# A hybrid layer on one core: both output projections with split operands, two tiles at once while the weights come, and x turned inside the second projection

## The reference

```python
mixed = jnp.concatenate([y.astype(x.dtype) * jax.nn.silu(z) for y, z in branches], axis=-1)
return x + mixed @ w_out                  # mixed 2048 x 1280, w_out 1280 x 1024
```

## Time and profile before

| | |
|---|---|
| three runs | 5369.63, 5380.27, 5392.05 us; median 5380.27 |
| the profiled execution | 5369.74 us, its span 5368.1 us |
| TensorE busy over the span | 4420.3 us, 82% |
| DVE, ACT, POOL busy | 2632.6, 1913.5, 738.0 us |
| `po`, first DMA to last product | 2516.99 to about 2844.6 us |
| second projection, first to last product | 2860.6 to about 3514.6 us |
| `pf`, first DMA to last product | 5117.41 to about 5357.5 us |
| POOL remainder of a weight block of `pf` | 2.34 us |

### The profile page before, as it was taken

The page is one execution under the profiler, slowest core; times in us unless marked ns, Lnnn a source line. Parts: engine busy times, 40 slices in busy tenths (PEclk is TensorE's granted clock), DMA queues, the critical chain, the costliest instruction groups (busy, mean ns, idle before and its releaser), DMA issues. The chain is left out here.

```text
span 5368.1 us, 64565 instructions
## 1 busy us (share of the span) xinstructions
PE 4420.3 (82%) x23178; PEld 3238.0 (60%) x23178; DVE 2632.6 (49%) x5352; ACT 1913.5 (36%) x3894; POOL 738.0 (14%) x753
## 2 busy tenths in 40 slices
PE   7988999973678888987998999956688887876668
PEld 6876777762566666665446888833344454544557
DVE  3114444445555544542111111148998888887435
ACT  3112233234223223332111010123676767777511
POOL 3101111100000000000000000012222333444310
PEclk9998999975667677776999999976587887877779
DMA  5336666643010000001221212120000001011032
GB/s 180 124 123 231 210 209 216 215 155 123 24 34 23 23 23 12 23 14 69 85 84 69 81 65 81 54 61 23 17 19 18 18 18 36 18 36 36 30 129 103
DMA packets 199360, 417.95 MB, mean 78 GB/s; under 512 B 37032, under 2 KB 67404, under 8 KB 198876
## 3 DMA queue, kind: packets, MB, share of 16 engines
q1 hardware_dynamic: 199040, 413.81, 22.5%
HBM read 292.08 MB, written 121.65 MB: 77 GB/s over the span
## 5 line engine op out<-in xcount | busy, mean ns | idle before, releaser
L3131 POOL TENSOR_TENSOR ds_E<-ds_bT 128x256 f32<-128x256 f32 x112 | 71.8, 641 | 2928.5 <-ACT ds_bT L3100 2743.2
L2620 PE MATMUL ds_big<-ds_ikT,ds_iqT 64*128 64x512 f32 (+3 forms) x640 | 384.0, 747 | 94.9 <-ACT ds_iqT L2597 60.2
L272 PE MATMUL g_acc<-g_ws_hi,second_hT_hi 128*128 128x512 f32 (+1 forms) x1024 | 384.5, 375 | 11.8 <-DVE g_ws_lo L307 11.8
L273 PE MATMUL g_acc<-g_ws_lo,second_hT_hi 128*128 128x512 f32 (+1 forms) x1024 | 384.2, 375 | 0.0
L274 PE MATMUL g_acc<-g_ws_hi,second_hT_lo 128*128 128x512 f32 (+1 forms) x1024 | 384.1, 375 | 0.0
L475 PE MATMUL mm_big<-mm_gw_hi,mm_ghT_hi 128*128 128x512 f32 (+1 forms) x768 | 318.5, 415 | 31.2 <-PEq L134 31.2
L2683 DVE TENSOR_SCALAR_CACHE_REDUCE ds_eq<-ds_hi,ds_num 128x2048 uint16<-128x2048 uint16 (+13 forms) x224 | 331.3, 1479 | 26.2 <-issue 4.0
L286 DVE COPY g_stage<-g_acc 128x512 f32<-128x512 f32 (+1 forms) x64 | 41.6, 650 | 529.0 <-PE g_acc L274 529.0
L477 PE MATMUL mm_big<-mm_gw_hi,mm_ghT_lo 128*128 128x512 f32 (+1 forms) x768 | 299.7, 390 | 0.0
L476 PE MATMUL mm_big<-mm_gw_lo,mm_ghT_hi 128*128 128x512 f32 (+1 forms) x768 | 299.3, 390 | 0.0
L2723 ACT ACTIVATE ds_signs<-ds_lo,ds_at 128x2048 bf16<-128x2048 uint16 (+13 forms) x224 | 291.4, 1301 | 1.5 <-issue 0.4
(11 more groups left out here) (505 smaller groups left out, 10007.3 us busy)
## 6 DMA issues: line engine op xcount, KB each, us to landing
mm_ghT_hi<-turned SPq DMA_DIRECT2D x96, 512.0 KB, 4.0
mm_ghT_lo<-turned SPq DMA_DIRECT2D x96, 512.0 KB, 5.3
proj<-g_stage SPq DMA_DIRECT2D x112, 256.0 KB, 2.0
proj<-mm_gstage SPq DMA_DIRECT2D x80, 256.0 KB, 5.0
mm_x<-proj SPq DMA_DIRECT2D x64, 256.0 KB, 3.8
g_w<-in_w_in SPq DMA_DIRECT2D x56, 256.0 KB, 4.0
proj<-fp_stage SPq DMA_DIRECT2D x48, 256.0 KB, 2.0
mm_graw<-in_w_in SPq DMA_DIRECT2D x40, 256.0 KB, 6.5
```

Of the source, the lines that this page charges most:

```text
L272: pe.matmul(sums, hT.hi[:, k, tile], wt.hi[:, k, 0:width], start=(k == 0), stop=False)
L273: pe.matmul(sums, hT.hi[:, k, tile], wt.lo[:, k, 0:width], start=False, stop=False)
L2620: pe.matmul(big[:, n % 2, 0:wd], iqT[o, h // 2], b.ikT[o, x:x + wd], start=True, stop=True)\
```

## The change

- `project_out` uses the split form for both `po` and `pf`. The weight blocks pass through the three slots of the row buffer `x` (new line 2378), ACT rounds them, DVE (no longer POOL) takes the remainder, and a slot is loaded again after that. `wo`, `mT` and the POOL part are gone.
- The columns of a tile have two buffers `m`, their turned and split form `mS` two buffers too; `keep` and `rest` now run for tile u + 2 while tile u is added.
- While the weights come, TensorE multiplies tiles 0 and 1 together: for each block k, when its remainder is there, the six products of tile 0 and the six of tile 1. Tile 2 is turned before the last group of blocks.
- SP issues the columns of tile 1 after the first weight block, and after the last remainder the rows of tiles 0 and 1, the columns of tile 2 and the rows of tile 2; from there columns of u + 3, store of u, rows of u + 3.
- `po` no longer turns x. `second_projection` (in place of `gemm`) loads x2 in half rows of 512 columns from memory into three slots `xt`, and in group 0 turns and splits tile t + 1 before it multiplies tile t.
- The eight weight blocks of the second projection's first group are loaded to `raw` by `po` after tile 4 (`ahead`), and `po` waits for them at its end.

```diff
-def gemm(nc, c, hT, w, out, groups, name, pad):
+def second_projection(nc, c, x, w, out, groups, raw):
...
+        hT = Split(B, "hT", [P, KD, SEQ])
+        xt = B.sb("xt", [P, 3, D_MODEL // 2])
+        tp = B.ps("tp", [P, 2, KD // 2, P])
...
+                def half_rows(v):
+                    t, c0 = v // 2, v % 2 * 512
+                    if v >= 3:
+                        sp.wait_ge(s.turned, v - 2)
+                    sp.dma_start(xt[:, v % 3], x[t * P:(t + 1) * P, c0:c0 + 512]).then_inc(x_in[v % 3], 16)
+                for v in range(5):
+                    half_rows(v)
...
+                        if g == 0:
+                            for v in range(2 * t + 7 if t else 5, min(2 * t + 9, 2 * TILES)):
+                                half_rows(v)
...
+                def turn(t):
+                    for half in range(2):
+                        v = 2 * t + half
+                        pe.wait_ge(x_in[v % 3], 16 * (v // 3 + 1))
+                        if t:
+                            pe.wait_ge(s.x_lo, 2 * (t - 1) + half + 1)
+                        for k in range(4):
+                            m = pe.transpose(tp[:, half, k], xt[:, v % 3, k * P:(k + 1) * P], c.ident)
+                        m.then_inc(s.turned, 1)
+                turn(0)
...
+                        if g == 0 and t + 1 < TILES:
+                            turn(t + 1)
+                        if g == 0:
+                            pe.wait_ge(s.x_lo, 2 * (t + 1))
...
+            def tile_hi(act, t):
+                for half in range(2):
+                    act.wait_ge(s.turned, 2 * t + half + 1)
+                    act.activation(hT.hi[:, 4 * half:4 * half + 4, t * P:(t + 1) * P], tp[:, half], ACT.Copy)\
+                       .then_inc(s.x_hi, 1)
+            def tile_lo(dve, t):
+                for half in range(2):
+                    place = (slice(None), slice(4 * half, 4 * half + 4), slice(t * P, (t + 1) * P))
+                    dve.wait_ge(s.x_hi, 2 * t + half + 1)
+                    dve.tensor_tensor(hT.lo[place], tp[:, half], hT.hi[place].bitcast(F32), ALU.subtract)\
+                       .then_inc(s.x_lo, 1)
...
+                        if g == 0 and k in (4, 7):
+                            tile_hi(act, (k - 4) // 3)
...
+                        for u in (t + 2, t + 3) if g == 0 and t + 3 < TILES else ():
+                            tile_hi(act, u)
...
-def project_out(nc, c, mix, w_out, x_old, x_out, name, turned_out=None, ln=None):
+def project_out(nc, c, mix, w_out, x_old, x_out, name, ln=None, ahead=()):
...
+    def passed(u, b):
+        return 2 * b + u + 1 if u < 2 else (nb - 1) * u + b + 1
...
-        wo = B.sb("wo", [P, K if not ln else 2, D_MODEL])
-        if ln:
-            ws = Split(B, "ws", [P, K, D_MODEL])
-            mS = Split(B, "mS", [P, K, P])
-        m = B.sb("m", [P, K * P])
         x = B.sb("x", [P, 3, D_MODEL])
-        mT = mS.hi if ln else B.sb("mT", [P, K, P])
+        ws = Split(B, "ws", [P, K, D_MODEL])
+        mS = Split(B, "mS", [P, 2, K, P])
+        m = B.sb("m", [P, 2, K * P])
...
+                def columns(u):
+                    if u >= 2:
+                        sp.wait_ge(s.turned, nb * (u - 1))
+                    sp.dma_start(m[:, u % 2], mix[u * P:(u + 1) * P, :]).then_inc(m_in[u % 2], 16)
+                def rows(u):
+                    if u >= 3:
+                        sp.wait_ge(stored[u % 3], 16 * (u // 3))
+                    sp.dma_start(x[:, u % 3], x_old[u * P:(u + 1) * P, :]).then_inc(x_in[u % 3], 16)
                 def store(u):
                     sp.wait_ge(s.summed, u + 1)
                     sp.dma_start(x_out[u * P:(u + 1) * P, :], x[:, u % 3]).then_inc(stored[u % 3], 16)
+                columns(0)
+                for k in range(K):
+                    if k >= 3:
+                        sp.wait_ge(s.w_lo, k - 2)
+                    sp.dma_start(x[:, k % 3], w_out[k * P:(k + 1) * P, :]).then_inc(w_in[k % 3], 16)
+                    if k == 0:
+                        columns(1)
+                sp.wait_ge(s.w_lo, K)
+                rows(0)
+                rows(1)
+                columns(2)
+                rows(2)
+                for dst, src in loads:
+                    sp.dma_start(dst, src).then_inc(s.par_in, 16)
                 for u in range(TILES):
-                    if u:
-                        sp.wait_ge(s.turned, nb * u)
-                    sp.dma_start(m[:], mix[u * P:(u + 1) * P, :]).then_inc(s.m_in, 16)
-                    if u == 0:
-                        for k in range(0 if ln else K):
-                            sp.dma_start(wo[:, k], w_v[:, k]).then_inc(w_in[k // 4], 16)
-                        for k in range(K if ln else 0):
-                            if k >= 2:
-                                sp.wait_ge(s.w_lo, k - 1)
-                            sp.dma_start(wo[:, k % 2], w_v[:, k]).then_inc((s.wa_in, s.wb_in)[k % 2], 16)
-                    if u >= 3:
-                        store(u - 3)
-                        sp.wait_ge(stored[u % 3], 16 * (u // 3))
-                        if not ln:
-                            sp.wait_ge(s.x_turned, 2 * (u - 2))
-                    sp.dma_start(x[:, u % 3], x_old[u * P:(u + 1) * P, :]).then_inc(x_in[u % 3], 16)
-                    if u == 1:
-                        for dst, src in loads:
-                            sp.dma_start(dst, src).then_inc(s.par_in, 16)
-                for u in range(TILES - 3, TILES):
+                    if u + 3 < TILES:
+                        columns(u + 3)
                     store(u)
+                    if u + 3 < TILES:
+                        rows(u + 3)
+                    if u == 4:
+                        for dst, src in ahead:
+                            sp.dma_start(dst, src).then_inc(s.ahead_in, 16)
...
-                    pe.wait_ge(s.m_in, 16 * (u + 1))
+                    pe.wait_ge(m_in[u % 2], 16 * (u // 2 + 1))
...
-                            pe.wait_ge(s.kept_lo if ln else s.kept, nb * (u - 1) + b + 1)
+                            pe.wait_ge(s.kept_lo, nb * (u - 1) + b + 1)
                         for k in range(kn):
-                            t = pe.transpose(tp[:, b, k], m[:, (k0 + k) * P:(k0 + k + 1) * P], c.ident)
+                            t = pe.transpose(tp[:, b, k], m[:, u % 2, (k0 + k) * P:(k0 + k + 1) * P], c.ident)
...
+                def products(u, k):
+                    for n in range(2):
+                        cols, sums = slice(n * 512, (n + 1) * 512), acc[:, u % 2, n]
+                        pe.matmul(sums, mS.hi[:, u % 2, k], ws.hi[:, k, cols], start=(k == 0), stop=False)
+                        pe.matmul(sums, mS.hi[:, u % 2, k], ws.lo[:, k, cols], start=False, stop=False)
+                        t = pe.matmul(sums, mS.lo[:, u % 2, k], ws.hi[:, k, cols], start=False, stop=(k == K - 1))
+                    return t
+                turn(0)
+                turn(1)
+                for b, (k0, kn) in enumerate(KB):
+                    if b == nb - 1:
+                        turn(2)
+                    pe.wait_ge(s.kept_lo, nb + b + 1)
                     for k in range(k0, k0 + kn):
+                        pe.wait_ge(s.w_lo, k + 1)
+                        for u in range(2):
+                            t = products(u, k)
+                            if k == k0 + kn - 1:
+                                t.then_inc(s.passed if b < nb - 1 else s.prod, 1)
+                for u in range(2, TILES):
                     if u + 1 < TILES:
                         turn(u + 1)
+                    pe.wait_ge(s.added, u - 1)
+                    for b, (k0, kn) in enumerate(KB):
+                        pe.wait_ge(s.kept_lo, nb * u + b + 1)
+                        for k in range(k0, k0 + kn):
+                            t = products(u, k)
+                        t.then_inc(s.passed if b < nb - 1 else s.prod, 1)
...
+                def keep(u):
+                    for b, (k0, kn) in enumerate(KB):
+                        act.wait_ge(s.turned, nb * u + b + 1)
+                        if u >= 2 and b < nb - 1:
+                            act.wait_ge(s.passed, passed(u - 2, b))
+                        elif u >= 2:
+                            act.wait_ge(s.prod, u - 1)
+                        act.activation(mS.hi[:, u % 2, k0:k0 + kn], tp[:, b, 0:kn], ACT.Copy).then_inc(s.kept, 1)
                 if ln:
                     act.preload_act_table_set(LN_EXP)
+                keep(0)
+                for k in range(K):
+                    act.wait_ge(w_in[k % 3], 16 * (k // 3 + 1))
+                    act.activation(ws.hi[:, k], x[:, k % 3], ACT.Copy).then_inc(s.w_hi, 1)
+                    if k == 0:
+                        keep(1)
...
+                def rest(u):
+                    for b, (k0, kn) in enumerate(KB):
+                        dve.wait_ge(s.kept, nb * u + b + 1)
```

(25 more changed lines are left out.)

119 lines of the change are left out of this document (22 added, 97 removed).

## The result

The kernel after takes 5291.1 us (median of four runs, 5282.5 to 5301.1), the kernel before in the same comparison 5379.2 us. The ratio is 0.9829, with a 95% interval of 0.9805 to 0.9853: 92 us less, between 79 and 105 (the two medians lie 88 us apart). The forecast was 5282 with a range of 5250 to 5314, from a sum of 92.9 us saved.

A forecast was written before the change was run, and what follows sets the result against it. TensorE's instructions were taken to bound steady state, and first operands the stage edges. Savings of 65.3 us in the first two stages and 27.6 in `pf` make 92.9 us, forecast 5282 us, range 5250 to 5314.

The forecast's parts named there:

- Product form: In `po`, three split products of 0.227 us replace one of 0.858: 0.177 us saved on each of 320, 56.6 us.
- Start of `po`: First product 10.2 us after the first DMA, 1.8 us stall before tile 2, first two tiles done at 41.8 us.
- The hinge: Between `po` and the second projection: next step begins at 252.8 us, its first product comes at 260.0 us.
- Transposes in the first group: x's transposes moved into the second projection: 12.3 us back, plus waits taken as 6.0 us (bounds 0 and 14).
- `pf`: Last projection: first product at 9.5 us instead of 34.3, a new wait of 9.5 us, 27.6 us saved in all.
- The sum: Whole kernel: 65.3 us net of the first two stages plus 27.6 us in `pf`, 92.9 us saved.
- rival 2: In the changed stages, the new waits don't come: saving 110 us, time 5265; chance 0.13.
- rival 1: Transfers come later than taken (half rows after 4 us, weight blocks over 2.7 apart): saving 70 us, 5305; chance 0.17.
- Rival 4: Products of `po` stay at the lower clock, 0.429 instead of 0.227 us each: time 5475; chance 0.02.

## Why the prediction was right

**Product form.** Right, and the largest term. 0.177 us on each of 320 was read as 56.6 us; undone it cost 52.3, because the full form also fills a wait that the split form has. The steady tile was forecast at 14.7 us and is 14.72. By the rule of the Trainium skill ("FP8 and Floating Point Precision", TensorE Precision Notes) on four passes for full FP32 the term was 68.6. The trace does not bear that out as a measure of time: 3.54 us a tile, 0.177 for each pair of block and half, side with the rows.

**Start of `po`.** First product forecast at 10.2 us, measured 10.2. The wait before tile 2 was put at 1.8 us and is 2.23. The pair was to end at 41.8 us and ends at 44.1. What was left out of the sum is the low clock after that wait: 24 products take from 2560.94 to 2568.12, 7.2 us, where 24 x 0.227 is 5.4. The low clock was booked in `pf`, for a wait of 9.5 us, but not here for one of 2.

**The hinge.** From the last store's issue to the next step 4.7 us were taken and 3.25 measured; from there to the first product 7.2 and 7.5. The first half row was taken at 2.7 us and its transposes begin 3.04 us after its issue. The 2.6 us estimated beside it rest on a fit of the Trainium skill ("DMA: Bandwidth & Descriptors", Anatomy of one DMA) that the section gives for DMAs of the GpSimd path; these are SyncE's.

**Transposes in the first group.** 12.3 + 6.0 = 18.3 us were forecast, 22.1 came. The wait was found at the place named, tile 5, at 5.59 us instead of 4.7. A tile of the group takes 6.34 us, 0.90 more than 5.44, so 12.6 us for fourteen. The largest mis-sized term is the low clock after the wait, taken as 1.3: the next tile's turning stands 8.59 us after the late one, 2.5 us more than its 0.66 and 5.44 us (in other executions with the same wait 1.7 to 2.2 more). It and the longer wait are 2.1 of the 3.8 us by which the forecast was short; 0.3 are the 12.6, and some 0.6 lie in small waits before later tiles. The rest is not traced. The stores ahead of the odd half rows were said to cost nothing at 3 us of landing; in the trace the landing is 3.6 us in the median, so this cover was just short (the earlier half rows gave 3.9 us, part of them from waits that the spreading had made).

**`pf`.** First product 9.5 forecast, 9.4 measured; wait 9.5 forecast, 8.57 measured; end of the pair 45.6 forecast, 45.6 measured (5109.16 - 5063.59); wait for tile 4's columns 3.3 forecast, 1.90 measured; the whole 27.6 less forecast, 26.1 measured. That the pair's end agrees to a tenth is partly luck: the columns came 0.5 us sooner than taken, and what follows them took 14.7 us for 14.3. Behind the second wait the low clock, which was not booked, made the next tile 1.7 us longer (13.45 for 11.78), and the products of tile 2 had waited 0.46 us for the sums of tile 0; together this is more than the 1.4 us by which the wait was taken too long:

```profile
5121.00:5124.00 3.00, 1.10 (x6) 0.64 (x5) 2.77 (x3) 0.04 (x1) 0.00 (x0) 1.00 0.66 262
5124.00:5128.00 4.00, 4.00 (x16) 3.33 (x15) 3.32 (x6) 1.19 (x2) 0.00 (x0) 0.57 0.35 135
```

**The sum** was 92.9 us; in the profiled executions the changed stages gave 86. All three parts were forecast too good, by 1.6 us up to the second projection, 3.8 in it and 1.5 in `pf`, each time with a low clock behind a wait that was left out or taken too short. By ratio 92 were measured, but that is known only to within 13 us, so this agreement to 1 us is luck. The predicted 5282 was 9 us low: 5 us because it started under the median of before, from which it would be 5287, and the rest is within the spread. The range's lower end is mis-added: 0.2% under rival 2's 5265 is 5254, not 5250; nothing hangs on it.

**Rivals.** None of the five took place as a whole; rival 1 had its part in the landing of half rows. Rival 4, the lower clock in `po`, is excluded by 1.00 over 202 us.

What stays open: how far the third weight slot alone, or the second buffer of `mS` alone, would carry `pf` was not tried; its first product 24.9 us sooner and its tiles 1.27 us shorter are read from the rows, and no run undoes the one without the other. Nor was it tried to keep x's transposes in `po` with split products, and so the 22.1 us of the first group were not set against what they would cost there.

## What to carry to other kernels

When TensorE gets its operands by one in-order DMA queue, list for each load what stands ahead of it and what its issue waits for, and compare with the moment of use: three misplaced loads cost this kernel 17 us by the ratios and 25 by the stages, and moving a fourth gave 4 more. Doing two tiles at once while weights come pays only as far as nothing else is wanted sooner by it; with the queue in the wrong order it cost 13 us in one stage (11 where the clock does not fall at tile 4), in the right one it gave 1.6 there. Price a wait on TensorE with the low clock behind it: here 1.8, 2.5 and 3.0 us behind the waits of 2.23, 5.59 and 8.57 us. Behind waits of about two microseconds it may come or not, in executions of the same code, so give it a range.

## What the runs showed of the hardware that was not expected

Idle times of about 2 us were followed by the lower clock in some executions and not in others. In `po`, behind 2.23 us, the products start 0.43 us apart and the granted clock is 0.63 over the four microseconds that follow; it fell in the same place behind 2.20 us in the kernel whose weights are not loaded ahead. At tile 4 of `pf` it fell in the kernel after (1.90 us idle, then 0.57 over four microseconds), in the kernel without the early weights (1.90) and in the one with the new `pf` alone (2.00). It stayed at 1.00 behind the same wait with early columns (1.96 us), with the remainders on POOL (1.90), with full-form products in `po` (2.05) and with spread weights (2.27). The length of the wait does not tell the two cases apart. Each fall cost about 1.6 us there: the tile behind it took 13.45 us where it took 11.85 in the others.

The many waits of the kernel without the pair, up to 1.49 us, left the clock at the upper level in `po`, with TensorE busy for 11.6 of these 16 us:

```profile
2548.00:2564.00 16.00, 11.64 (x47) 8.09 (x46) 7.33 (x6) 6.08 (x6) 0.00 (x0) 1.00 0.58 189
```
